# A hybrid transformer kernel: its first modulation in two halves, delta-net key products at another place, table loads and head finish reordered

## The reference

```
mod = silu(c) @ ada_w[i] + ada_b[i]            # 6 x 1024: shift, scale, gate; twice
u   = x * (1 + mod[1]) + mod[0]                # modulate
y   = mixer(u)                                 # attention, delta net or linear attention
x   = layer_norm(a * x + mod[2] * y) ; h = modulate(x) ; x = layer_norm(a * x + mod[5] * conv_glu(h))

# gated delta net, per head and chunk, state S (128 x 128), forward and backward scan:
T      = (I + strict_lower(beta * K K^T * decay))^-1
v_new  = T (beta * V) - T (beta * K * exp(gc)) S
o      = (Q * exp(gc)) S + (Q K^T * decay) v_new
S      = S * exp(g_last) + (K * exp(g_last - gc))^T v_new
# then o = rms_norm(o) * norm_w * silu(gate), and o @ w_o
```

## Time and profile before

| what | value |
|---|---|
| median of 3 runs | 2898.62 us (2896.61 to 2898.7) |
| the profiled execution, its own time | 2901.96 us |
| span in the profile | 2899.9 us |
| mean granted TensorE clock | 0.956 of 2.4 GHz |
| busy: PE, DVE, ACT, POOL | 91%, 41%, 27%, 56% |
| the delta net's loop | 983 to 1176 us |

### The profile page before, as it was taken

How to read it: one execution, slowest core, us unless ns; L and a number is a source line. 1 busy time by engine, 2 the same in 40 slices (tenths; PEclk the granted TensorE clock), 3 DMA queues, 4 the chain that set the end, 5 groups by cost and what they waited for, 6 DMA issues and landing times. The chain is left out here.

```text
span 2899.9 us, 45667 instructions
## 1 busy us (share of the span) xinstructions
PE 2652.6 (91%) x16461; PEld 2132.3 (74%) x16461; DVE 1183.2 (41%) x2197; ACT 788.1 (27%) x1490; POOL 1626.6 (56%) x1665
## 2 busy tenths in 40 slices
PE   6988999999898899899999999898999998888987
PEld 4766677787687788767778668886677786767886
DVE  2364322222469667432222320674322223443455
ACT  2253322210541433132211140441322113243311
POOL 3402566665657222466667556775666575607985
PEclk8999999999899989899999999999999999999998
DMA  6333455422222000255542222002555322203442
GB/s 236 117 117 117 155 172 173 151 87 87 61 73 87 16 2 1 73 173 173 173 132 87 73 76 88 16 1 89 188 174 174 116 88 72 88 1 116 159 145 87
DMA packets 217162, 305.60 MB, mean 105 GB/s; under 512 B 7332, under 2 KB 155551, under 8 KB 217024
## 3 DMA queue, kind: packets, MB, share of 16 engines
q1 hardware_dynamic: 179007, 228.16, 23.9%
q10 hardware_dynamic: 38016, 75.50, 8.0%
HBM read 302.60 MB, written 1.05 MB: 105 GB/s over the span
## 5 line engine op out<-in xcount | busy, mean ns | idle before, releaser
L588 POOL TENSOR_TENSOR w_lo<-w_raw,w_hi 128x512 fp32r<-128x512 f32 x720 | 948.5, 1317 | 108.2 <-POOL w_hi L585 88.1
L585 POOL TENSOR_SCALAR w_hi<-w_raw 128x512 fp32r<-128x512 f32 x720 | 472.1, 656 | 871.9 <-PE bank L1055 609.4
L1055 PE MATMUL bank<-u_lo,w_hi 128*128 128x512 f32 (+1 forms) x2144 | 810.3, 378 | 43.9 <-DVE u_lo L1725 21.5
L1055 PE MATMUL bank<-u_hi,w_lo 128*128 128x512 f32 (+1 forms) x2144 | 791.7, 369 | 0.0
L1055 PE MATMUL bank<-u_hi,w_hi 128*128 128x512 f32 (+1 forms) x2144 | 791.6, 369 | 0.0
L1055 PEld LDWEIGHTS bank<-u_lo,w_hi 128*128 128x128 f32 x2144 | 408.8, 191 | 182.9 <-issue 99.3
L1055 PEld LDWEIGHTS bank<-u_hi,w_hi 128*128 128x128 f32 x2144 | 408.7, 191 | 68.5
L1055 PEld LDWEIGHTS bank<-u_hi,w_lo 128*128 128x128 f32 x2144 | 409.4, 191 | 63.0
L1633 PE MATMUL bank<-gs_lo,w_hi 128*128 128x512 f32 (+1 forms) x576 | 212.2, 368 | 9.4 <-DVE gs_lo L2339 6.1
L1633 PE MATMUL bank<-gs_hi,w_lo 128*128 128x512 f32 (+1 forms) x576 | 211.1, 366 | 0.0
L1633 PE MATMUL bank<-gs_hi,w_hi 128*128 128x512 f32 (+1 forms) x576 | 211.1, 366 | 0.0
(11 more groups left out here) (334 smaller groups left out, 3859.6 us busy)
## 6 DMA issues: line engine op xcount, KB each, us to landing
w_raw<-in_ffn_w_up SPq DMA_DIRECT2D x88, 1024.0 KB, 7.1
ada_w<-in_ada_w ACTq DMA_DIRECT2D x72, 1024.0 KB, 5.2
w_raw<-in_ffn_w_down SPq DMA_DIRECT2D x44, 1024.0 KB, 4.9
ada_w<-in_ada_w SPq DMA_DIRECT2D x16, 1024.0 KB, 5.1
w_raw<-in_gdn_w_in SPq DMA_DIRECT2D x16, 1024.0 KB, 5.7
w_raw<-in_attn_w_qkv SPq DMA_DIRECT2D x12, 1024.0 KB, 5.3
w_raw<-in_gla_w_in SPq DMA_DIRECT2D x12, 1024.0 KB, 5.3
ada<-in_ada_w SPq DMA_DIRECT2D x8, 1024.0 KB, 13.5
```

Of the source, the lines that this page charges most:

```text
L585: eng.tensor_scalar(w_hi[:, q, :], src, 1.0, 0.0, ALU.mult, ALU.add).then_inc(pool.own, pool.step())
L588: eng.tensor_tensor(w_lo[:, q, :], src, w_hi[:, q, :].bitcast(F32), ALU.subtract).then_inc(w_split, 1)
L1055: mm = eng.matmul(bank[banks[m]][:, T], w[:, q, c:c + P], v[:, k, T], start=(k == 0 and n == 0), stop=(k == KT - 1 and n == 2))
```

## The change

1. The `ada_w` units come in the order of blocks 0, 2, 1, 3. PE does blocks 0 and 2 (`ada_blocks(0)`), DVE writes shift and scale of tiles 0 to 3 (`modulation_first(0)`), ACT and DVE make these four tiles of u, PE multiplies the first half of attention unit 0, does blocks 1 and 3 (`ada_blocks(1)`), and the same follows for tiles 4 to 7. SP loads unit 0 between the two halves of `ada_w` and unit 1 behind them. The slots of `ada_w` lie elsewhere, since u is now written while they are in use.
2. The masks are loaded last of the start's transfers, and cast by DVE before the low part of the last tile of u; the wait for the constants counts 17 DMAs in place of 18.
3. In the delta net's loop PE does the key-state product of d = 0 (`key_state(0)`) behind a32 and that of d = 1 behind b32; DVE copies b32 before it computes y.
4. In the two rounds of the last token tile (s = 3) the key transposes, decayed keys, state products and state updates are left out; waits for them wait for the outputs in their place.
5. ACT's load of the Sqrt table (`root_table`) stands at the head of a norm and of a head finish.
6. In the head finish DVE gates four tiles, takes the reciprocal, and gates the others between the multiplications.

The diff, cut to its core:

```diff
+ADA_ORDER = (0, 2, 1, 3)
...
                 eng.dma_start(gdp[:, n, :], w.rearrange("o d h -> o (d h)").to_broadcast([P, 2 * B_HEADS])).then_inc(s_con, 16)
-            eng.dma_start(msk_f[:].rearrange("p a b -> p (a b)"), a["masks"]).then_inc(s_con, 16)
             rowv = lambda t, pat: t.rearrange(pat, p=P)
...
             for n in range(ADA_FIRST):
+                if n == ADA_FIRST // 2:
+                    load(column(a["attn_w_qkv"][0], 0))
                 if n >= ADA_SLOTS:
                     eng.wait_ge(ada_done, sp.next(ada_done))
-                src = ada_half(0, n % 2, slice(n // 2 * ADA_N, (n // 2 + 1) * ADA_N))
+                c = ADA_ORDER[n // 2] * ADA_N
+                src = ada_half(0, n % 2, slice(c, c + ADA_N))
                 eng.dma_start(k4(ada_0[:, n % ADA_SLOTS, :]), src).then_inc(ada_0_loaded[n % ADA_SLOTS], 16)
+            load(column(a["attn_w_qkv"][0], 256))
+            eng.dma_start(msk_f[:].rearrange("p a b -> p (a b)"), a["masks"]).then_inc(msk_loaded, 16)
             for l in range(LAYERS):
...
                 if KIND[l] == "attn":
-                    for n in range(6):
+                    for n in range(2 if l == 0 else 0, 6):
                         load(column(a["attn_w_qkv"][slot], n * 256))
...
                     for hg in range(2):
-                        if (s, hg) != (0, 0):
+                        if (s, hg) == (TT - 1, 1):
+                            eng.wait_ge(od_ready, 14)
+                        elif (s, hg) != (0, 0):
                             eng.wait_ge(s_done, pool.next(s_done, 2))
...
                             eng.tensor_tensor(E[:], E[:], bq[:, hg * 4:hg * 4 + 4, tl * P:(tl + 1) * P], ALU.mult).then_inc(qd_ready, 1)
-                eng.wait_ge(s_done, pool.next(s_done, 2))
+                eng.wait_ge(od_ready, 16)
...
                 for t in range(KT):
+                    if (l_aff, w, t) == (0, 0, 0):
+                        eng.wait_ge(mod_first, act.next(mod_first))
+                    if (l_aff, w, t) == (0, 0, 4):
+                        eng.wait_ge(mod_ready, act.next(mod_ready))
                     if first_u[0] < 2:
...
                             Dm, E = bt[d][0:2]
-                            if not first:
+                            if (s, hg) == (TT - 1, 1):
+                                eng.wait_ge(od_ready, 14)
+                            elif not first:
                                 eng.wait_ge(s_done, act.next(s_done))
...
                 eng.wait_ge(ty_ready, act.next(ty_ready, 2))
-                eng.wait_ge(s_done, act.next(s_done, 2))
-                eng.wait_ge(st_upd, act.next(st_upd))
+                eng.wait_ge(bo_ready, 16)
...
                 tiles = [t for h in heads for t in h]
+                root_table()
                 for i, t in enumerate(tiles):
...
+            def root_table():
+                eng.wait_ge(act.own, act.count())
+                eng.activation(warm[:], con[:, K_COL:K_COL + 1], ACT.Sqrt).then_inc(act.own, act.step())
...
                 strips = slice(S.start // P * 32, P)
+                root_table()
                 eng.wait_ge(ms_ready, act.next(ms_ready))
...
-                eng.wait_ge(act.own, act.count())
-                eng.activation(warm[:], con[:, K_COL:K_COL + 1], ACT.Sqrt).then_inc(act.own, act.step())
                 eng.wait_ge(var_ready, act.next(var_ready))
...
                            ACT.Silu).then_inc(st_ready, 1)
-            eng.wait_ge(mod_ready, act.next(mod_ready))
             make_u(0, 0, 0)
...
                     delta_net()
-                    eng.wait_ge(st_upd, act.next(st_upd, 16))
+                    eng.wait_ge(st_upd, act.next(st_upd, 13))
                     head_finish(bo, [(h,) for h in range(B_HEADS)], B_HD)
...
                     column_unit(u_hi, u_lo, (0, 1) if n % 2 == 0 else (2, 3), T if n < 4 else slice(0, TOK),
-                                first=u_tile if n == 0 else None)
+                                first=(first_tile if l == 0 else u_tile) if n == 0 else None)
                     for m in (2 * n - 2, 2 * n - 1):
...
                         for d in range(2):
-                            if not first:
+                            if not first and (s, hg) != (TT - 1, 1):
                                 eng.wait_ge(st_upd, pe.next(st_upd))
...
                             mm.then_inc(kq_ready, 1)
-                        if first:
-                            eng.wait_ge(st_upd, pe.next(st_upd))
-                        for d in range(2):
+                        def key_state(d):
+                            if first and d == 0:
+                                eng.wait_ge(st_upd, pe.next(st_upd))
                             if not first:
...
                             mm.then_inc(a_ready, 1)
+                        key_state(0)
                         for d in range(2):
...
                             mm.then_inc(b_ready, 1)
+                        key_state(1)
                         for d in range(2):
...
                             mm.then_inc(a_ready, 1)
-                        for d in range(2):
+                        for d in range(2 if s < TT - 1 else 0):
                             for b in range(4):
...
                             mm.then_inc(od_ready, 1)
+                            if s == TT - 1:
+                                continue
                             eng.wait_ge(kdm_ready, pe.next(kdm_ready))
...
                 eng.wait_ge(bo_ready, pe.next(bo_ready, 2))
-                eng.wait_ge(st_upd, pe.next(st_upd, 2))
...
+            def ada_blocks(h):
+                for n in range(4 * h, 4 * h + 4):
+                    ada_unit(n % 2, ada_0, n % ADA_SLOTS, ada_0_loaded[n % ADA_SLOTS])
+                    if n % 2 == 1:
+                        ada_turn(ADA_ORDER[n // 2])
...
+            def first_tile(k):
+                if k == KT // 2:
+                    ada_blocks(1)
+                u_tile(k)
...
             eng.wait_ge(st_ready, pe.next(st_ready))
-            for n in range(ADA_FIRST):
-                if n >= 2 and n % 2 == 0:
-                    ada_turn(n // 2 - 1)
-                ada_unit(n % 2, ada_0, n % ADA_SLOTS, ada_0_loaded[n % ADA_SLOTS])
-            ada_turn(ADA_FIRST // 2 - 1)
+            ada_blocks(0)
             for l in range(LAYERS):
...
+            def modulation_first(h):
+                for j in (4 * h, KT + 4 * h):
+                    mod_add(0, j, j + 4, bank[6][:, 2 * j:2 * j + 8]).then_inc(dve.own, dve.step())
+                eng.wait_ge(dve.own, dve.count())
+                t = slice(4 * h, 4 * h + 4)
+                eng.tensor_scalar(aff[:, 0, 0, t, :], mod[:, 0, KT + 4 * h:KT + 4 * h + 4, :], 1.0, None, ALU.add).then_inc(dve.own, dve.step())
+                eng.tensor_copy(aff[:, 0, 1, t, :], mod[:, 0, t, :]).then_inc(dve.own, dve.step())
+                eng.wait_ge(dve.own, dve.count())
+                eng.sem_inc(mod_ready if h else mod_first, 1)
...
                         for d in range(2):
+                            TTm = bt[d][4]
+                            eng.wait_ge(b_ready, dve.next(b_ready))
+                            i, o = slice(96 * d, 96 * d + 32), slice(32 + 32 * d, 64 + 32 * d)
+                            eng.tensor_copy(bT[o, :, i], quad(bank[3 * d + 1][o, :])[:, :, i])
+                            for q in range(2):
+                                i, o = slice(64 * q + 32 * d, 64 * q + 32 * d + 32), slice(64 * q + 32 - 32 * d, 64 * q + 64 - 32 * d)
+                                ins = eng.tensor_copy(TTm[i, :, o], quad(bank[3 * d + 2][i, :])[:, :, o])
+                            ins.then_inc(t_ready, 1)
+                        for d in range(2):
                             Dm = bt[d][0]
...
                             TTm = bt[d][4]
-                            eng.wait_ge(b_ready, dve.next(b_ready))
-                            i, o = slice(96 * d, 96 * d + 32), slice(32 + 32 * d, 64 + 32 * d)
-                            eng.tensor_copy(bT[o, :, i], quad(bank[3 * d + 1][o, :])[:, :, i])
-                            for q in range(2):
-                                i, o = slice(64 * q + 32 * d, 64 * q + 32 * d + 32), slice(64 * q + 32 - 32 * d, 64 * q + 64 - 32 * d)
-                                ins = eng.tensor_copy(TTm[i, :, o], quad(bank[3 * d + 2][i, :])[:, :, o])
-                            ins.then_inc(t_ready, 1)
-                        for d in range(2):
-                            TTm = bt[d][4]
                             i, o = slice(64 * d, 64 * d + 64), slice(64 - 64 * d, 128 - 64 * d)
...
                             eng.tensor_copy(TTm[i, :, o], quad(bank[3 * d + 2][i, :])[:, :, o]).then_inc(t_ready, 1)
-                        for d in range(2):
+                        for d in range(2 if s < TT - 1 else 0):
                             eng.wait_ge(tr_ready, dve.next(tr_ready))
...
```

(49 more changed lines are left out.)

## The result

The kernel after takes 2856.7 us (median of 4 runs, 2854.51 to 2859.31) against 2898.66 before (4 runs): the ratio is 0.9854, with a 95% interval from 0.9837 to 0.9871, or 42 us less. The forecast was 2866.2 with a range from 2858 to 2882. The direction was right, and so was what was said of the loop and of the norms; what was said of the two finishes was wrong.

The account below looks back on a forecast made before the run. PE, busy 91% of the span, was taken as the bound. Terms 0 + 9.6 + 5.7 + 14 + 4.2 - 1.1 = 32.4 us off 2901.96 left 2869.6, or 2866.2 on the median's scale; range 2858 to 2882.

Parts of the forecast that it names:

- The clock: Delta net's loop: key-state products fill PE's thin stretch, so most dips to half clock go; 14 us less, bounds 0 and 17.
- The order: Delta net's loop: reordered products and copies bring a64 of d = 1 earlier, 1.2 us in each of 8 rounds; 9.6 less.
- Rival (d): Delta net's loop: copies of b64 wait for all of y, 2.15 us paid a round; slower, 2907; chance 0.03.
- The last tile: Delta net's last two rounds: transposes, state products and state update left out; 5.7 us less.
- The norms: Six norms lose the table load between variance sums and root, 0.7 us each; 4.2 us less, bounds 3.5 and 6.
- The start: Up to attention unit 0: x lands 1 us earlier, second modulation half comes late; 0 us, bounds +4.5 and -4.
- Rival (b): Start: clock falls during ada_w blocks between the halves, unit 0 ends at 66; 4 us more, 2870; chance 0.10.
- The finishes: Behind both scans: delta net gains 1.1 us, linear attention loses 2.2; together 1.1 us slower, bounds +2 and -4.
- Two gates (2.4) then lie before the first low part: Head finishes: after the early reciprocal, two of DVE's gates at 1.2 us each still precede the first low part.
- The load does lie on the path: Head finishes: ACT reaches the table load only when outputs are there, so all squares start 1.5 us later.
- Rival (a): Delta net's loop: the clock dips as before; gain only 18.4 us, 2880; chance 0.34.
- (c): Delta net's loop: dips stay and order gives at most 0.5 us a round; gain 12.8, 2886; chance 0.03.

Follow-up runs that it names:

- e12: The kernel after, with the finishes' Sqrt table load ahead of ACT's waits and GpSimd's split held until DVE's reciprocal; 2858.61 us.
- e8: The kernel after, with the Sqrt table load put ahead of ACT's waits at the end of both scans; 2854.25 us.
- e2: The kernel before with point 4 alone (nothing computed for the state behind the last token tile); 2897.04 us.
- e1: The kernel before with point 3 alone (key-state products and DVE's copies of b32 reordered); 2875.54 us.
- e6: The kernel before, with the query product of d = 0 repeated each round between b32 and a64, result unread; 2881.65 us.

## Why the prediction came out too small

- **The clock, 14: right in kind, 2.6 short.** With 1.09 a round from the order and 6.0 from the last tile, 16.6 of the loop's 31.3 are left for the clock. The term had taken 1.5 off for a dip brought in from before the loop and 2.7 for one round's worth. The kernel after comes into its loop at the full clock, and one dip stayed, that of the last round, worth 1.4: without the load the round takes 19.54, and the same round takes 18.14 at a clock of 1.00 in e12. Why it dips in the kernel after and in e8 and not in e12 is open.
- **The order, 9.6: 8.7.** 21.82 less 20.73 is 1.09 for each of 8 rounds, 1.2 predicted. y ended 0.2 before the copies of b64, 0.3 predicted. Rival (d) had its place right and its price was never due.
- **The last tile, 5.7: 6.0** in e2, where the two rounds ran partly at the lower clock, and 5.4 at the full clock.
- **The norms, 4.2: 4.15.** No drain behind the table load, as the row had said.
- **The start, 0: 1.0.** x came 1.9 earlier, 1 was taken. Rival (b) did not occur: PE ran the second blocks at the full clock (1.93 for a pair at 42.07, as at 23.18), straight behind the first half of the unit; a dip followed them, from 51.6 to 58.3.
- **The finishes, -1.1: +5.6. This is the step that failed**, with 6.7 of the 9.5 us by which the forecast missed. "Two gates (2.4) then lie before the first low part" carried the price of a gate, 1.2, from where GpSimd splits to where it does not. Behind the linear attention, rows to projection took 7.99 in place of the 10.0 that I reckoned: 2 x (2.4 - 1.41). "The load does lie on the path" was charged twice and due once: 1.4 more. The 1.3 for a dip was not due: the clock rose to 1.00 at 1935.7, 4.7 us ahead of the projection. These three make the linear attention's finish +2.6 where I had -2.2. Behind the delta net the two gates disappeared behind PE, which in both kernels spreads rows for 6.11 us before the projection, at a mean clock of 0.72: the gain is the whole 4.23 by which the rows start earlier, less the load, +2.8 where I had +1.1. (Counted to the next norm's mean, the two finishes give the 5.6.)
- **Unchanged code, 0: 1.7**, not to be told from chance (below).

The errors, in this order: +2.6 - 0.9 + 0.3 + 0 + 1.0 + 6.7 + 1.7 = 11.4. The sum was 32.4, the spans of the pair differ by 43.7, and their own times by 43.97. On the medians the difference is 42. Rival (a), the dips as before, got 0.34 and is refuted by e1 and e6; (c) with it.

The range ended too high. The two bounds that it names for its lower end, 3 us more from the clock and 1.8 from the norms, give 2861.4 and not 2858; and the bounds of the finishes (+2 and -4) didn't hold the case that the gates are cheaper elsewhere, although the trace before showed it: there GpSimd's split ended at 1184.3, and the last two of DVE's eight gates, from 1184.80 on, took 1.40 together.

## What to carry to other kernels

A mean duration has a partner: before it is carried to another place, look at which engine ran beside it there, above all VectorE instructions with two SBUF inputs beside GpSimd. Where TensorE's clock dips in a stretch of small products, try to move real work into it, or, failing that, to repeat a product: in this loop, where TensorE waited anyway, it cost nothing (rounds of 21.82 with it and without). A table load with its one-element activation belongs ahead of all waits for the data; in e8 that gave 1.4 us in its place.

## What the runs showed of the hardware

- One product (8 matmuls, 1.16 us), made a second time in each of eight rounds of some 24 us, took 17 us off the kernel (e6), by the clock alone. In the rounds that dipped before, PE's longest pause in the thin stretch is 0.68, as in the one that did not.
- Beside GpSimd's split, an instruction of DVE on 128 x 512 with two SBUF inputs takes 1.2 us on average in place of 0.67; a low part up to 1.78 in place of 0.68; the cast of the masks 2.25 in place of 1.15.
- ACT's table load does not wait for what its ACTIVATE waits for: at 1906.56 it ran 19 us ahead of its `warm`. Behind the delta net it did wait, at 1141.03; that several waits precede it there is the likely reason. Put ahead of them all it ran 9.5 us before the squares (e8), but a single wait in that place was not tried.
- The same instructions take different times from kernel to kernel, by when the clock dips: from ACT's copy of a bank at 108.47 (107.50 after) to the first mean, 201.89 us in the kernel after, 205.34 before, and 202.9 to 207.4 in the twelve experiments, with no order that the edits explain. In e8, whose start is that of the kernel after, it was 207.41. A single pair of traces thus carries some 3 us in code that nobody touched.
